# Reordering the instruction queues around the sparse-attention branch of a hybrid encoder block

## The reference

```
q, k = rotary(rms_norm(q_b)), rotary(rms_norm(k_b))        # 8 heads of 128
score = sum_h relu(q_idx . k_idx) * w                      # the indexer, 8 heads of 64
idx   = top_k(score where admissible, 128)                 # per query
p     = softmax(q . k / sqrt(128) over the chosen keys)
y_b   = (p @ v) * silu(z_b)
x     = x + (sum_b sigmoid(gate_b) * (y_b @ w_branch_b)) @ w_out
```

## Time and profile before

| what | us |
| --- | --- |
| median of 3 runs (range) | 974.56 (973.63 to 976.5) |
| the profiled execution, its own time | 974.56 |
| its span | 972.5 |
| PE busy | 957.4, 98% of the span |
| DVE, ACT, POOL busy | 715.0, 534.5, 341.4 |
| mean granted clock of PE | 0.998 |
| `m_scale_p` of the last M head ends; PE starts `m_turn_p` | 218.2; 219.7 |
| products 0, 1, 2, 3, 4 of pair 0 start | 234.3, 238.5, 242.6, 246.8, 251.3 |
| product 6 of pair 0, `f_panel(0, 0)` start | 262.7, 268.2 |
| product 0 of pair 1 (behind its `b_turn_qk`) starts | 308.0 |
| `f_panel(1, 0)`, `f_panel(3, 0)` start | 342.1, 489.1 |
| `branch_panel(0)`, `(1)`, `(2)` start | 502.4, 530.0, 563.0 |

### The profile page before, as it was taken

How to read it: one execution, slowest core, us unless ns; L and a number is a source line. 1 busy time by engine, 2 the same in 40 slices (tenths; PEclk the granted TensorE clock), 3 DMA queues, 4 the chain that set the end, 5 groups by cost and what they waited for, 6 DMA issues and landing times.

```text
span 972.5 us, 13407 instructions
## 1 busy us (share of the span) xinstructions
PE 957.4 (98%) x4897; PEld 840.3 (86%) x4897; DVE 715.0 (74%) x1079; ACT 534.5 (55%) x810; POOL 341.4 (35%) x247
## 2 busy tenths in 40 slices
PE   8999999999899999999998999999999999999998
PEld 6888888888888988988977878898998989988887
DVE  6878987687986686696696476796776867734586
ACT  6877645454356546546553321676675857741351
POOL 0100834457037036036030053271623626106600
PEclk9999999999999999999999999999999999999999
DMA  8624222143432531532353234707034150638312
GB/s 272 249 87 130 88 87 87 43 138 123 148 102 65 161 101 65 152 109 66 119 217 130 99 128 153 238 12 215 2 89 138 32 152 1 235 92 311 142 44 86
DMA packets 105156, 119.27 MB, mean 123 GB/s; under 512 B 4772, under 2 KB 80136, under 8 KB 104332
## 3 DMA queue, kind: packets, MB, share of 16 engines
q1 hardware_dynamic: 105084, 118.53, 37.2%
q10 hardware_dynamic: 16, 0.00, 0.0%
HBM read 106.45 MB, written 12.07 MB: 122 GB/s over the span
## 4 chain that ended last, share of the span: by engine, by line
PE 87%; DVE 8%; issue 2%; ACT 1%; DMA 1%; POOL 0%; SPq 0%; DVEq 0%; ACTq 0%
PE proj L780 39%; PE proj L1289 9%; PE proj L1140 9%; PE att L1310 7%; PE proj L1310 5%; PE att L1360 3%; PE proj L950 2%; PE att L1122 2%; PE att L1104 1%; DVE score L2396 1%; PE att L1069 1%; DVE small L2394 1%; PE proj L1246 1%; PE att L1112 1%; PE att L1047 1%
## 5 line engine op out<-in xcount | busy, mean ns | idle before, releaser
L780 PE MATMUL proj<-hT_hi,w_hi 128*128 128x512 f32 x328 | 129.0, 393 | 0.0
L780 PE MATMUL proj<-hT_hi,w_lo 128*128 128x512 f32 x328 | 128.0, 390 | 0.0
L780 PE MATMUL proj<-hT_lo,w_hi 128*128 128x512 f32 x328 | 127.8, 390 | 0.0
L2131 DVE TENSOR_TENSOR w_lo<-w_raw,w_hi 128x2048 fp32r<-128x2048 f32 x28 | 68.9, 2462 | 49.6 <-ACT w_hi L1410 45.6
L1410 ACT ACTIVATE w_hi<-w_raw 128x2048 fp32r<-128x2048 f32 x28 | 53.6, 1914 | 67.7 <-PE proj L780 66.4
L780 PE MATMUL proj<-y_hi,w_hi 128*128 128x512 f32 x192 | 76.1, 397 | 5.0 <-DVE merged L2665 3.3
L780 PE MATMUL proj<-y_hi,w_lo 128*128 128x512 f32 x192 | 75.4, 393 | 0.0
L780 PE MATMUL proj<-y_lo,w_hi 128*128 128x512 f32 x192 | 75.4, 393 | 0.0
L780 PEld LDWEIGHTS proj<-hT_hi,w_lo 128*128 128x128 f32 x328 | 61.6, 188 | 13.1
L780 PEld LDWEIGHTS proj<-hT_lo,w_hi 128*128 128x128 f32 x328 | 61.7, 188 | 12.3
L780 PEld LDWEIGHTS proj<-hT_hi,w_hi 128*128 128x128 f32 x328 | 61.6, 188 | 12.2
(11 more groups left out here) (522 smaller groups left out, 2931.1 us busy)
## 6 DMA issues: line engine op xcount, KB each, us to landing
w_raw<-w_in_in SPq DMA_DIRECT2D x36, 512.0 KB, 4.3
w_raw<-w_in_in SPq DMA_DIRECT2D x56, 256.0 KB, 3.4
w_raw<-w_branch_in SPq DMA_DIRECT2D x10, 1024.0 KB, 5.0
merged<-w_in_in SPq DMA_DIRECT2D x38, 256.0 KB, 3.6
merged<-w_in_in SPq DMA_DIRECT2D x14, 512.0 KB, 6.0
w_raw<-w_in_in SPq DMA_DIRECT2D x6, 1024.0 KB, 5.8
w_raw<-w_mem_kv_in SPq DMA_DIRECT2D x10, 512.0 KB, 7.1
yF<-x_in SPq DMA_DIRECT2D x8, 512.0 KB, 7.9
```

The source lines that it names most:

```text
L780: ins = mm(ps, lhs[a](k, k0), rhs[b](k, k0), start=(first and k == 0 and j == 0), stop=(last and k == KH - 1 and j == 2))
L2131: V.tensor_tensor(w_lo[:, kh, :, 0:n], w_raw[:, kh, :, 0:n], w_hi[:, kh, :, 0:n].bitcast(F32), ALU.subtract).then_inc(w_lo_done, 1)
```

## The change

Nothing is added to or taken from the arithmetic; instructions change places in the queues, and some waits change with them. SP issues the first load of slot c before d, and the reload of `yb_kept` earlier. PE does `b_turn_qk(l)` at the head of `f_panel(i, 1)` and not at the head of the next pair, and r's hooks one to three slots earlier. For that `b_turn_qk` of an odd head waits for r's maxima only, and `b_turn_p(r)` now waits until q and k of head l have been copied out of att0 and att1. ACT and DVE follow with `b_qk_high(l)` and `b_qk_low(l)` between r's exponentials and r's probabilities. DVE does `b_rotary(r)` before `b_low(n + 8)`, `b_low(n + 10)` before `b_maxes(r)`, and the top-k rounds in other places: before pair 0 stand now 8 rounds over 384 keys and 4 over 256, where 4 over 384 stood, and 4 remain inside pair 0, where 12 were. ACT does `m_exps` of the last M head before three splits. GpSimd starts the weight sums of the next pair, the squares of head l and the sums of line 3074 on earlier conditions.

```
 SP   unit_load("b", 0); wait s_low 3
+     unit_load("c", 0)
      unit_load("d", 0)
-     unit_load("c", 0)
 ...
      sp.wait_ge(f_half, HALF0 + 2 * PAIRS - 1)
+     sp.dma_start(yF[:, 0:6 * S], yb_kept).then_inc(late_landed, 16)
      sp.wait_ge(b_rotated, B_HEADS - 1)
      ...
-     sp.dma_start(yF[:, 0:6 * S], yb_kept).then_inc(late_landed, 16)
 PE   def b_turn_qk(a):
-         pe.wait_ge(*((b_pcopied, a * 4) if a else (m_y, 2 * M_HEADS)))
+         if a == 0:      pe.wait_ge(m_y, 2 * M_HEADS)
+         elif a % 2:     pe.wait_ge(b_masked, a * 4)
+         else:           pe.wait_ge(b_pcopied, a * 4)
      def b_score(a):
          if a: pe.wait_ge(b_y, a)
+               pe.wait_ge(b_pcopied, a * 4)
      def b_turn_p(a):
+         if a % 2 == 0:
+             pe.wait_ge(b_qcopied, a + 2)
+             pe.wait_ge(b_kcopied, a + 2)
      def b_unit(i):
-         if i: b_turn_qk(tail)
      f_panel(i, 0):
-         {3: [turn_qk(r)], 5: [score(r)]}
+         {2: [turn_qk(r)], 4: [score(r)]}
      f_panel(i, 1):
-         {3: [turn_p(r)], 5: [values(r)]}
+         {0: [turn_qk(l)], 1: [turn_p(r)], 3: [values(r)]}
      branch_panel(0):
-         {1: [score(r)], 5: [turn_p(r)], 7: [values(r)]}
+         {1: [score(r)], 2: [turn_qk(l)], 4: [turn_p(r)], 6: [values(r)]}
      branch_panel(1):
-         {0: [turn_qk(l)], 2: [score(l)], 5: [turn_p(l)], 7: [values(l)]}
+         {0: [score(l)], 3: [turn_p(l)], 5: [values(l)]}
 ACT  b_body(i):
-         if i: b_qk_high(tail)          # first
          ...  b_exps(r); b_high(n + 11)
+         b_qk_high(l)
          b_probs_high(r)
      before the pairs:
+     m_exps(M_HEADS - 1)
      bs_split(2), bs_split(0), bs_split(1)
-     m_exps(M_HEADS - 1)
      after the pairs: b_exps(r)
+     b_qk_high(l)
      b_probs_high(r); split_hi(GB[0] + 1, 0, ...); b_values_high(l)
-     b_qk_high(l)
 DVE  b_body(i):
-         if i: b_qk_low(tail)           # first
          b_low(n + 2)
-         rounds(1, 4)                   # 4 rounds over 256 keys, pair 0 only
          b_maxes(tail); b_low(n + 3); b_add(i, 1, ...); b_scale_p(tail)
-         rounds(2, 2)                   # rounds over 384 keys, pair 0 only
          b_low(n + 4); b_probs(tail)
-         rounds(2, 2)
          b_low(n + 5); b_low(n + 6); b_finish(tail)
-         rounds(2, 4)
+         in pair 0: 4 rounds over 384 keys; make_masks()
          b_add(i, 3, ...); b_low(n + 7)
-         if i == 0: make_masks()
          b_add(i, 5, ...)
+         b_rotary(r)
          b_low(n + 8)
-         b_rotary(r)
          b_values_low(r); b_low(n + 9); b_qk_low(r); b_rotary(l)
+         b_low(n + 10)
          b_maxes(r)
-         b_low(n + 10)
          b_scale_p(r); b_low(n + 11)
+         b_qk_low(l)
          b_probs(r); b_low(n + 12); b_finish(r); b_values_low(l)
      before the pairs (M's last head):
      m_norms
+     1 round over 384
      bs_low_of(2), bs_low_of(0), bs_low_of(1); m_scale_p
-     2 rounds over 384
+     1 round over 384
      m_probs
+     2 rounds over 384
      b_low(0); m_rest; bs_low_of(3); b_low(1)
-     2 rounds over 384
+     4 rounds over 384; 4 rounds over 256
      after the pairs: b_maxes(r); ym_low(4..7)
+     b_qk_low(l)
      b_scale_p(r); ... b_finish(r); b_values_low(l)
-     b_qk_low(l)
 POOL b_early_sums(i):
-         if i: pool.wait_ge(op_low, B_OPS * i + 1)
      b_squares(a), a odd:
-         pool.wait_ge(b_rotated, a)
+         pool.wait_ge(b_norm_steps, a * 3 - 1)
      before line 3074:
-     pool.wait_ge(ys_lo, 2 * KT)
+     pool.wait_ge(b_y, B_HEADS)
```

More of the change, by code:

```diff
@@ L1089, in b_turn_qk @@
                 pe.wait_ge(b_rotated, a + 1)
-                pe.wait_ge(*((b_pcopied, a * 4) if a else (m_y, 2 * M_HEADS)))
+                if a == 0:
+                    pe.wait_ge(m_y, 2 * M_HEADS)
+                elif a % 2:
+                    pe.wait_ge(b_masked, a * 4)
+                else:
+                    pe.wait_ge(b_pcopied, a * 4)
                 for c in range(2):
@@ L1146, in b_unit @@
                 tail = 2 * i - 1
-                if i:
-                    b_turn_qk(tail)
                 b_product(i, 0, h_block(0, 0), main, True,
@@ L1199, in _ @@
                 if i < PAIRS - 1:
-                    f_panel(i, 0, (0, P, 2 * P), {3: [lambda: b_turn_qk(r)], 5: [lambda: b_score(r)]})
-                    f_panel(i, 1, (0, P, 2 * P), {3: [lambda: b_turn_p(r)], 5: [lambda: b_values(r)]})
+                    f_panel(i, 0, (0, P, 2 * P), {2: [lambda: b_turn_qk(r)], 4: [lambda: b_score(r)]})
+                    f_panel(i, 1, (0, P, 2 * P), {0: [lambda: b_turn_qk(l)], 1: [lambda: b_turn_p(r)], 3: [lambda: b_values(r)]})
                 else:
@@ L1228, in _ @@
             pe.wait_ge(u_added, 6 * PAIRS)
-            branch_panel(0, y_split(1), {1: [lambda: b_score(r)], 5: [lambda: b_turn_p(r)], 7: [lambda: b_values(r)]})
-            branch_panel(1, None, {0: [lambda: b_turn_qk(l)], 2: [lambda: b_score(l)], 5: [lambda: b_turn_p(l)],
-                                   7: [lambda: b_values(l)]})
+            branch_panel(0, y_split(1), {1: [lambda: b_score(r)], 2: [lambda: b_turn_qk(l)], 4: [lambda: b_turn_p(r)],
+                                         6: [lambda: b_values(r)]})
+            branch_panel(1, None, {0: [lambda: b_score(l)], 3: [lambda: b_turn_p(l)], 5: [lambda: b_values(l)]})
             branch_panel(2, y_split(2))
@@ L1767, in b_body @@
                 tail, r, l = 2 * i - 1, 2 * i, 2 * i + 1
-                if i:
-                    b_qk_high(tail)
                 b_high(n + 2)
@@ L2560, in b_body @@
                 tail, r, l = 2 * i - 1, 2 * i, 2 * i + 1
-                def rounds(t, times):
-                    for _ in range(times if i == 0 else 0):
-                        top_round(t)
-                if i:
-                    b_qk_low(tail)
                 b_low(n + 2)
-                rounds(1, 4)
                 if i:
@@ L2584, in b_body @@
                     b_finish(tail)
-                rounds(2, 4)
+                else:
+                    for _ in range(4):
+                        top_round(2)
+                    make_masks()
                 b_add(i, 3, (banks[0], banks[1]), b_fifth, 5)
                 b_low(n + 7)
-                if i == 0:
-                    make_masks()
                 b_add(i, 5, (banks[2], banks[3]), b_second, 3)
+                b_rotary(r)
                 b_low(n + 8)
-                b_rotary(r)
                 b_values_low(r)
@@ L2612, in _ @@
             m_scale_p(M_HEADS - 1)
+            top_round(2)
+            m_probs(M_HEADS - 1)
             for _ in range(2):
                 top_round(2)
-            m_probs(M_HEADS - 1)
             b_low(0)
@@ L2619, in _ @@
             b_low(1)
-            for _ in range(2):
+            for _ in range(4):
                 top_round(2)
+            for _ in range(4):
+                top_round(1)
             for i in range(PAIRS):
@@ L3021, in b_early_sums @@
             def b_early_sums(i):
-                if i:
-                    pool.wait_ge(op_low, B_OPS * i + 1)
                 pool.wait_ge(raw_landed["b"], B_LOADS * i + 48)
```

## The result

The kernel after takes 1018.4 us (median of 4 runs, 1015.78 to 1019.99), the kernel before 974.1 beside it (972.72 to 976.5): a ratio of 1.0449, 95% interval 1.0417 to 1.0483. The forecast was 1014 in a range of 991 to 1026. The profiled execution took 1016.72, its span is 1014.6 (972.5 before), the mean granted clock of PE 0.983 (0.998 before).

A forecast was written before the change was run, and what follows sets the result against it. PE, busy 98% of the span, was taken as the bound, so every new wait is paid in full. 1.1 + 2.7 + 11.4 + 2 x 9.5 + 5.4 = +39.6 on 974.6 gave 1014 us, range 991 to 1026.

The forecast's parts named there:

- rival B: PE's clock also falls behind the new waits; seven could cost 1.7 us each, +12 on the forecast, 1026; chance 0.25.
- Before pair 0 (+1.1): Ahead of pair 0, `m_scale_p` ends at 220.7 instead of 218.2, so PE waits 1.1 us.
- Pair 0 (+2.7): Up to `f_panel(0, 0)`: new waits 8.4 us, old ones gone 4.6; 2.7 more beyond the 1.1 before it.
- Slot 2 (0.95): In pairs 1 and 2, turn_qk(r) waits 0.95 us for rotary, slowed beside head l's squares.
- Slot 0 (5.0, bounds 0.6 to 5.0): Second panel, pairs 1 and 2: turn_qk(l) waits 5.0 us for the maxima, DVE alternating with GpSimd's early sums.
- Slot 1 (3.55): Second panel, pairs 1 and 2: turn_p(r) waits 3.55 us for qk_low(l), 7.15 after the maxima.
- Pair 3 and branch panels (+5.4): From pair 3 on: +1.2 to `branch_panel(0)`, -3.65 in the first two branch panels, +7.8 at `branch_panel(2)` from GpSimd's sums.
- the +1.2 to `branch_panel(0)`: In pair 3, `b_low(n + 8)` behind rotary holds slot 2 by 2.4 us; `branch_panel(0)` starts at F + 14.5, was F + 13.35.
- A (no alternation): DVE and GpSimd go side by side without delaying each other: +17 us, 991; chance 0.2.
- C: Faster: the moved hooks have slack after all and the old waits go: 967; chance 0.05.
- D: The waits cancel the gains, the pairs losing what the rest gives: 971.6 to 977.5; chance 0.02.
- The lock: GpSimd and two-SBUF-input DVE instructions hold shared ports throughout, giving the upper bounds; one power row spoke against it.

The follow-up runs named there:

- squares_wait: Kernel after, with GpSimd's squares of head l waiting again for head r's rotary: 1016.47 us, ratio 1.0442 to the kernel before.
- sums_wait: Kernel after, with GpSimd's early weight sums of the next pair waiting again for `b_low(n + 11)`: 1016.39 us, ratio 1.0437 to the kernel before.
- slot2: Kernel after, with turn_p(r) and values(r) one block later in `f_panel(i, 1)`: 1010.1 us, ratio 1.0373 to the kernel before.
- low8_first: Kernel after, with DVE's `b_low(n + 8)` ahead of `b_rotary(r)` again: 1020.97 us, ratio 1.0492 to the kernel before.
- runs 1 and 3: `hsums_wait` (1009.17 us) and `sums_wait` (1016.39 us), each the kernel after with one GpSimd wait put back.
- hsums_wait: Kernel after, with GpSimd's sums of line 3074 waiting again for all `yb_low`: 1009.17 us, ratio 1.0365 to the kernel before.
- turn_back: Kernel after, with turn_qk(l), qk_high(l) and qk_low(l) back at the head of the next pair, in the pairs only: 1011.95 us, ratio 1.0388.
- panels_only: Kernel before, with only turn_qk of head 7 moved into `branch_panel(0)` and `branch_panel(1)`'s hooks earlier: 968.47 us, ratio 0.9962.

## Why the prediction was right

**What bounds.** The mechanism held: PE is the bound, the new waits stand at the hooks that were forecast, and VectorE's queue, in two places ACT's, sets their end. The profile's waits show it, and the experiments that move one hook or one wait; that the table adds up to the span's 42.1 us does not, as it must. But not all of the time lies in waits, as the sum had it. PE's idle time (span less busy) grew by 26.5, from 15.1 to 41.6, and its busy time by 15.6, from 957.4 to 973.0, with the same 4897 matmuls, mostly because they ran slower behind the waits. In the pairs this is mostly the same time under another name, since the slowed PE arrives later at a wait that VectorE or ACT ends.

How close the total came is partly luck: one stage was 3.5 too low, and four others together 2.9 too high.

**The rows read.** Two readings of the earlier trace rows were wrong. Its first row says 3.3 us in two waits, the longest 2.2, and not one wait of 3.3; so rival B's case of half clock stood behind a wait of 2.2, shorter than the 2.8 behind which the clock stayed full. And 1.1 is not the third largest of PE's waits. The same list has three more, two of them far ahead of the changed code, and this one ahead of `branch_panel(0)`:

```profile
PE proj L780 <- DVE w_lo L2131: 1.4, 1, 1.4
```

The sum doesn't rest on either, since it took the stages' lengths (60.6 against 54.2).

**Before pair 0 (+1.1).** From the first matmul of `BS[0]` to m_turn_p 12.0 us (210.56 to 222.56), 10.9 before (208.76 to 219.65): 1.1.

**Pair 0 (+2.7).** 3.0. Counted from the same start, product 3 was forecast at 253.4 and came at 253.4 (255.18 less 1.8); product 2 waits 2.1 until `b_low(2)` is done at 247.7 (2.05; the list gives this wait to "issue"), `b_add` is waited for by 1.9 (1.7). Only the save's wait was 1.4 and not 3.4, and the rows of the clock say why:

```profile
244.00:252.00 8.00, 5.91 (x26) 5.62 (x26) 6.17 (x10) 0.00 (x0) 4.15 (x3) 0.82 0.17 51
```

Behind the 2.1 wait the matmuls of product 2 fell to half clock and took 1.6 longer, all of it taken from the wait that follows, which ACT ends.

**Slot 2 (0.95).** Turn_qk(r) was forecast at F + 6.4 and came at F + 6.34, a wait of 0.85. (In pair 0 the three waits were 2.8, 2.6 and 2.0, where 3.2, 5.0 and 3.55 were forecast; there too slowed blocks took the place of waiting, and the stage added 10.7 for 11.4.) Its reason, rotary stretched by head l's squares, is in the rows above; `squares_wait` takes it away.

**Slot 0 (5.0, bounds 0.6 to 5.0).** 4.17. The sums' data was forecast at F + 15.5 and landed at F + 15.8. DVE was stretched by 3.0, not 3.6. The choice of the upper bound was right in that the two engines do take turns, and `sums_wait` shows the wait falls to 1.0 when the sums are held back.

**Slot 1 (3.55).** The chain from the maxima to turn_p was forecast at 7.15 and is 7.2. The wait is 2.24 only because the slow clock behind slot 0 makes PE arrive 1.4 later; the sum is the same. `slot2` confirms that the chain sets it.

**Pair 3 and branch panels (+5.4).** The gain of 3.65 came (-1.0 with a new wait of 2.35 before `branch_panel(2)`, so -3.4 without), and GpSimd's sums cost 2.35 + 4.3 = 6.7, forecast 7.8. The wait of turn_qk(l) for the maxima was 1.05 and not 2.6; a slowed block and score ahead of it took 1.6. But the +1.2 to `branch_panel(0)` was 4.7. This is the one term that was far off. The forecast counted the wait for `b_low(n + 8)` and not what else hangs on it: SP's load of the first branch weights waits for that same instruction, and so do ACT's and DVE's split of them. SP's queue and ACT's, kernel after:

```profile
530.87 0.93 SPq L491 DMA_DIRECT2D w_raw<-w_branch_in  x2
```

```profile
535.92 1.92 ACT L1417 ACTIVATE w_hi<-w_raw 128x2048 fp32r<-128x2048 f32 x1 [10.00 <-issue]
...
538.83 1.28 ACT L1756 ACT_TABLE_LOAD   x1
540.12 0.60 ACT L1756 ACTIVATE sig<-proj 128x512 f32<-128x512 f32 x1
```

The load is issued at 530.87, behind rotary; ACT stands 10 us idle until its data is there, and its evacuation of the last gates, which `branch_panel(0)` waits for by 2.1, stands behind that split in its queue. In `low8_first`, which brings the load forward, `branch_panel(0)` comes 4.9 sooner behind `f_panel(3, 0)`.

**The rivals.** A (no alternation) is out: six stretched rows above, and runs 1 and 3. B (the clock falls too) was half right: it falls behind most long waits, but in the panels of pairs 0 to 2 keeping it up gave back 0.8 (in pair 2 it fell all the same), not the 1.7 per wait that the rival charged, because a later wait for DVE or ACT absorbs it. Where none follows it is paid: `sums_wait` lost 2.2 in pair 1 behind turn_p. The Trainium skill (TensorE: Matmul & The Clock Gate, Part 1) has the lower clock for an idle array; the windows agree where it fell, but it didn't fall behind every wait, and the price must be read on the path. C and D are out.

**The lock.** Two-operand VectorE instructions from SBUF took 1.4 to 2.9 us beside GpSimd's sums and squares and 0.6 to 0.7 alone, and the engines took turns instruction by instruction. The Trainium skill (SBUF — State Buffer, "SBUF: two separate sides") says that one of the pair holds the shared ports for its whole instruction; these rows agree. The power, 2.02 us of GpSimd at 358.78, again left rotary's four products beside it at 0.6 apart, which that rule doesn't give.

## What to carry to other kernels

When an engine that never waits is the bound, moving work earlier on it can only help where the feeding engines have slack at that very point: step the feeding queue from the last known-good row and compare it with the new time of need, hook by hook. Look at every wait in the code that names a moved instruction, loads on the DMA queue included; the term missed here was such a one. A GpSimd wait that looks needless may be what keeps it away from VectorE's critical stretch: it cost 0.1% to remove on the old order, and to remove its neighbour ahead of the sums of line 3074 cost 8 us on the new one. And split a change before judging it: two small moves in its manner, without the rest, give 0.8%.

## What the runs showed of the hardware

- A VectorE TENSOR_TENSOR of 128x512 with both operands in SBUF took 1.4 to 1.5 us beside GpSimd's sums of 128x384 or squares of 128x512, and 2.9 beside its sums of 128x1024; alone 0.68 to 0.69. VectorE instructions with one operand in PSUM (line 2667, four in 2.47 at 600.09, beside the fourth such sum) came 0.60 apart, as without it.
- A VectorE TENSOR_SCALAR of 128x4 took 0.97 beside a GpSimd sum, 0.16 otherwise: tiny instructions wait too.
- GpSimd lost less: four sums of 128x384 took 5.07 with VectorE beside them (kernel after) and 3.87 without (`sums_wait`); sums of 128x1024 came 2.8 apart beside VectorE's subtractions (kernel after) and 2.35 apart with VectorE idle (kernel before, from 569.42).
- Whether the clock falls behind a wait is not a matter of the wait's length alone. In the kernel before it fell behind a wait of 2.2 and not behind one of 2.8; `panels_only`, with the same 2.8 wait, has it fall there. Of nine profiles with the same code up to `f_panel(0, 0)`, the 2.0 to 2.5 us wait ahead of product 2 was followed by half clock in five (after, `hsums_wait`, `sums_wait`, `turn_back`, `slot2`) and by full clock in the other four. Where it stayed full there, the save's wait was 2.9 to 3.0 in place of 1.4 to 1.5, and in three of those four the clock fell behind that one instead, where nothing absorbs it. So from product 0 to `f_panel(0, 0)` the same code took 36.9 to 39.8 us. One of the three, `low8_first`, to set beside the row of pair 0 in the kernel after:

```profile
252.00:260.00 8.00, 7.89 (x30) 7.92 (x31) 3.13 (x2) 2.38 (x3) 0.00 (x0) 0.62 0.67 199
```

- At `branch_panel(2)` it is the same: from its start to branch A 47.9 to 48.0 us where the clock fell behind the first of its waits (after, `squares_wait`, `sums_wait`, `low8_first`), 49.6 where it fell behind the second (`turn_back`, `slot2`). Two profiles can differ by this alone.
